# The place of the value products in TensorE's queue, in the head loop of three fused attentions

## The chip, the cores and the metric

One core of one Trainium2 chip runs the whole program. The metric is the device time of one execution in microseconds, as the median of the runs. All times below that belong to one moment are microseconds from the start of the profiled execution's span.

## What is computed

A first block of two layers (short convolution and SwiGLU; dilated-group attention and a mixture of experts), and behind it a second block of two layers, on 256 tokens of width 1024, all in float32. The change lies in the attentions, of which there are three: one with 15 heads in the first block, and one with 16 heads in each layer of the second. Cut to one head, each computes:

```python
s = einsum('qd,kd->qk', q, k) * HEAD_DIM ** -0.5   # 256 x 256, head dimension 64
s = s + bias_or_mask                                # window, T5 table, neighbourhood, or causal dilation
p = softmax(s)                                      # (second block: six heads with a sink logit)
o = einsum('qk,kd->qd', p, v)
```

In the first block all heads are causal, so the first 128 queries need one tile of 128 keys and the others two. In the second block both query tiles have two key tiles. After the heads come a scaling, in the second block an RMS norm for each of three groups of heads, and the output projection.

## The kernel before

The program is written engine by engine, with an explicit queue for each (TensorE, ScalarE, VectorE, GpSimd, SyncE) and semaphores between them; nothing reorders it. What counts here is the function `attention` of TensorE, and the two functions of the same name of ScalarE and VectorE that work against it. Heads go in pairs p = 0, 1, ..., 7; the 16 heads of the second block go in the order 10, 1, 0, 11, 12, 3, 2, 13, 14, 5, 4, 15, 6, 7, 8, 9. Tiles are held two deep, one for each head of a pair: `ps` banks 4 and 5 for scores, `prob` for probabilities, `ps` banks 6 and 7 for transposed probabilities, `probT` for their copy in SBUF. Value products go to `ps` banks 0 to 3, where all heads' outputs stay until they are scaled.

TensorE, in turn p, issues: the scores of pair p (line 933; waits for `s_max`, the maxima of pair p-1), the transposes of pair p-1 (line 945; waits for `s_exp`, and for `s_pte` of the pair before it, since the bank is used again), and the value products of pair p-2 (line 960; waits for `s_pte`, the copy to SBUF).

ScalarE, in turn p: four exponentials (line 1410; waits for `s_max` of its head), in the first five turns the high half of one weight unit (line 436), then the two copies of the transposes (line 1422; each waits for `s_ptp`, the transposes of its head, and for `s_pv`, the value products of the head two before, which read the same `probT`). In the last turn of the second block's attentions there stand the exponential of the sinks (line 1641) and two square sums (line 1635) ahead of the copies.

VectorE, in turn p: for each head a pass over each query tile (line 1927) that adds scores and bias, writes `prob` and takes the maximum (waits for `s_sc_ps`, the scores, and for `s_ptp`, the transposes of the head two before, which read the same `prob`); for heads 0 to 3 of the second block a mask pass (line 1908) stands ahead of it. Then one or two accumulations of a later layer's modulation (line 1733), and in turns 1 to 5 the low half of one weight unit (line 440). After the last turn VectorE reduces the head statistics, scales the heads (lines 2103, 2342; waits for `s_pv`), and normalizes (from line 2355). SyncE issues the bias loads of a head four biased heads ahead, after `s_max`.

Of the kernel before, what the change touches and what calls it, by code (L numbers as in the profile page):

```python
# [24 lines left out]
P = 128  # L25
S = 256
T = S // P
# [175 lines left out]
def build(nc, g, out, ctx):  # L203
# [3 lines left out]
    def sem(name):  # L207
        return ctx.enter_context(nc.semaphore(name))
# [43 lines left out]
    prob = prob_both[:, 0:2 * T * S].rearrange("p (i t s) -> p i t s", i=2, t=T)  # L252
# [33 lines left out]
    ps = ctx.enter_context(nc.psum_tensor("ps", [P, 8, 512], F32))  # L286
    ident = table[:, C_ID:C_ID + P]
# [49 lines left out]
    s_sc_ps, s_max, s_exp = sem("scores_in_psum"), sem("max_ready"), sem("exp_done")  # L337
    s_ptp, s_pte, s_pv = sem("probT_in_psum"), sem("probT_out"), sem("pv_in_psum")
# [194 lines left out]
    def _(sp):  # L533
# [5 lines left out]
        def mods(n):  # L539

            for q in range(mod_at[0], mod_at[0] + n):
                m, _, k, third = MOD_ORDER[q]
                w = mod_source(m)[0]
                if q >= MOD_SLOTS:
                    sp.wait_ge(s_mused, q - MOD_SLOTS + 1)
                sp.dma_start(mod_in[:, q % MOD_SLOTS, :], w[k * P:(k + 1) * P, third * MOD_W:(third + 1) * MOD_W])\
                    .then_inc(s_min[q % MOD_SLOTS], 16)
            mod_at[0] += n
# [160 lines left out]
    def head_list(second):  # L709

        heads = []
        if not second:
            for h in range(H1):
                heads.append((h // 2, h % 2, 8 + h // 2, h % 2, 2 * W1 + h * HD))
            return heads
        for h in range(4):
            heads.append((h // 2, h % 2, 2 + h // 2, h % 2, 512 + h * HD))
        for grp, (c0, v0) in enumerate(((4, 1280), (8, 1920))):
            for h in range(6):
                kv = h // 3  # L720
                same = kv == h % 2
                heads.append((c0 + h // 2, h % 2, c0 + 3 if same else 12 + grp, h % 2, v0 + kv * HD))
        return heads

    def key_tiles(second, qt):
        return T if second or qt else 1


    def head_order(second):

        return HEAD_ORDER if second else tuple(range(H1))
# [10 lines left out]
    def _(pe):  # L742
# [167 lines left out]
        def beside_later(order, j):  # L910

            later = [h for h in order[j + 1:] if h // 8 == order[j] // 8]
            if order[j] + 1 in later:
                return 0, 1
            return (1, 0) if order[j] - 1 in later else (0, 0)

        def attention(a):

            second = a > 0
            heads, order = head_list(second), head_order(second)  # L920
            n, i0 = len(heads), HEADS_BEFORE[a]
            pe.wait_ge(s_qte, TRANS_BEFORE[a] + TRANS[a] // 2)
            width = QKV2 if second else QKV1
            pairs = (n + 1) // 2
            pair = lambda p: range(2 * p, min(2 * p + 2, n)) if 0 <= p < pairs else ()
            for p in range(pairs + 2):
                if p and p < pairs:
                    pe.wait_ge(s_max, i0 + 2 * p)
                for qt in range(T):
                    for i in pair(p):  # L930
                        qc, qh, kc, kh, _ = heads[order[i]]
                        nk = key_tiles(second, qt) * P
                        last = pe.matmul(ps[:, 4 + i % 2, qt * S:qt * S + nk],  # L933
                                         qkT[qh * HD:(qh + 1) * HD, qc, qt * P:(qt + 1) * P],
                                         qkT[kh * HD:(kh + 1) * HD, kc, 0:nk], start=True, stop=True)
                        if qt == T - 1:
                            last.then_inc(s_sc_ps, 1)
                for j in pair(p - 1):
                    pe.wait_ge(s_exp, i0 + j + 1)
                    if j >= 2:  # L940
                        pe.wait_ge(s_pte, i0 + j - 1)
                    for qt in range(T):
                        for kt in range(key_tiles(second, qt)):
                            at = (qt * key_tiles(second, 0) + kt) * P
                            last = pe.transpose(ps[:, 6 + j % 2, at:at + P],  # L945
                                                prob[:, j % 2, qt, kt * P:(kt + 1) * P], ident)
                    last.then_inc(s_ptp, 1)
                for j in pair(p - 2):
                    pe.wait_ge(s_pte, i0 + j + 1)
                    if second and j == n - 2:  # L950
                        pe.wait_ge(s_ho, 6 * (a - 1) + 2)
                    h = order[j]
                    v = heads[h][4]
                    left, right = beside_later(order, j)
                    for qt in range(T):
                        dst = ps[:, 2 * qt + h // 8, (h % 8 - left) * HD:(h % 8 + 1 + right) * HD]
                        nk = key_tiles(second, qt)
                        for kt in range(nk):
                            at = kt * width + v
                            last = pe.matmul(dst, probT[:, j % 2, qt * key_tiles(second, 0) + kt, :],  # L960
                                             qkv[:, at - left * HD:at + (1 + right) * HD],
                                             start=kt == 0, stop=kt == nk - 1)
                    last.then_inc(s_pv, 1)

        def y_transposes(a, first, end):

            for pair in range(first, end):
                pe.wait_ge(s_y, Y_BEFORE[a] + Y_READY[a][pair])
                for i in range(2):
                    c = Y_CHUNK(a, 2 * pair + i)  # L970
                    w = o_rows(c) if a == 0 else P
                    for t in range(T):
                        at = i * S + t * P
                        last = pe.transpose(ps[0:w, 4 + pair, at:at + P], xn[:, t, c * P:c * P + w], ident)
                last.then_inc(s_yTp, 1)
# [168 lines left out]
        pe.wait_ge(s_qa, 6)  # L1144
        pe.wait_ge(s_qd, 6)
        attention(0)
        y_transposes(0, 0, 4)
        project_out(fa, N_WO1, O_CHUNKS, o_rows, lambda k: (s_yTl, k + 1))
# [5 lines left out]
        for c in range(DC):  # L1154
            pe.wait_ge(s_htl, HT(3) + c + 1)
            pe.matmul(ps[0:2 * E, 0, 0:S], rw[:, c, :], hTh[:, c, :], start=c == 0, stop=False)
            last = pe.matmul(ps[0:2 * E, 0, 0:S], rw[:, c, :], hTl[:, c, :], start=False, stop=c == DC - 1)
# [14 lines left out]
        for t in range(T):  # L1172
            last = pe.matmul(ps[:, 1, t * E:(t + 1) * E], act[0:2 * E, 0, t * P:(t + 1) * P],
                             table[0:2 * E, C_ST:C_ST + E], start=True, stop=True)
# [79 lines left out]
        for l in range(2):  # L1254
            n0 = l * LAYER_UNITS
            s = 4 + 2 * l
            if l == 0:
                sum_cols(s)
            normed_T(s)
            q0, d0 = 6 + 4 * l, 6 + 3 * l  # L1260

            def first_pairs():
                pe.wait_ge(s_htl, HT(s + 1))
                pe.wait_ge(s_qa, q0 + 3)
                pe.wait_ge(s_qc, l + 1)
                qk_transposes(1 + l, 0, 3)

            project_in(fb, n0 + N_IN2, 4, 512, s, q0, d0, {(3, 2): first_pairs})
            sum_gate(s)
            pe.wait_ge(s_q, 3 + l)  # L1270
            qk_transposes(1 + l, 3, 6)
            pe.wait_ge(s_qa, q0 + 4)
            pe.wait_ge(s_qd, d0 + 3)
            qk_transposes(1 + l, 6, 7)
            pe.wait_ge(s_mga, s + 1)
            attention(1 + l)
            y_transposes(1 + l, 0, 2)
            project_out(fb, n0 + N_WO2, DC, lambda k: P, lambda k: (s_yTl, 2 * YT0[1 + l] + k + 1),
                        free=(s_ho, 6 * (l + 1)), beside=lambda: y_transposes(1 + l, 2, 4))
            sum_cols(s + 1)  # L1280
            normed_T(s + 1)
            first_ht = HT(s + 1)
            dense(fb, n0 + N_FFN2, l * STEPS, s + 1)
# [1138 lines left out]
```

## Time and profile before

| what | us |
|---|---|
| median of 3 runs | 1982.87 (1980.46 to 1987.34) |
| span of the profiled execution | 1978.7 |
| TensorE busy in the span | 1862.4 (94%) |
| VectorE busy | 1638.0 (83%) |
| ScalarE busy | 1141.5 (58%) |

The page gives no time for the profiled execution other than its span. A span runs from the first to the last recorded instruction; the device time of a run is somewhat longer. In the rows below PE is TensorE's matmul, PEld its weight load, DVE is VectorE, ACT ScalarE; L933 is line 933 of the kernel; `out<-in` are the tiles. In a timeline, the bracket at the end tells how long the engine sat idle before the instruction and who released it, and xN that N instructions of one line stand merged in it.

### The profile page before, as it was taken

The page shows a single profiled execution, that of the slowest core. Times are in us where ns is not written, and L with a number is a line of the kernel's source. Part 1 is how long each engine was busy: PE and PEld are TensorE (multiplying, and loading weights), DVE is VectorE, ACT ScalarE, POOL GpSimd, SP SyncE. Part 2 cuts the span into 40 slices and gives each one's busy share as a digit, 9 for nine tenths or more (in the row PEclk, how much of TensorE's full clock was granted, in tenths as well). Part 3 has the DMA queues.
Part 4 walks back from the last instruction along what each step waited for, and adds up shares of the span by engine and source line. Part 5 has one row for each costly group of instructions (what it writes and reads, how often), then busy time and mean ns, then how long its engine had stood idle before and what let it go on. Part 6 is the DMA issues. An engine that isn't in the chain of part 4 may idle for free.

```text
span 1978.7 us, 32211 instructions
## 1 busy us (share of the span) xinstructions
PE 1862.4 (94%) x10670; PEld 1603.6 (81%) x10670; DVE 1638.0 (83%) x2193; ACT 1141.5 (58%) x1616; POOL 36.1 (2%) x47
## 2 busy tenths in 40 slices
PE   3999998988999999999999999988799998889998
PEld 2989998866788888888888888866689997679997
DVE  7999995768999999999999989887887758887554
ACT  3445444454777777777777777754654435545443
POOL 2000000000000000000000000000000000000000
PEclk9999999999999999999999999988999999999999
DMA  9978995557799999999999999958478874845772
GB/s 326 352 250 308 384 365 154 172 177 244 261 343 359 344 361 341 359 341 360 341 361 341 360 341 359 339 191 244 142 234 279 283 262 148 245 159 189 224 222 80
DMA packets 368485, 551.26 MB, mean 279 GB/s; under 512 B 35827, under 2 KB 293110, under 8 KB 368342
## 3 DMA queue, kind: packets, MB, share of 16 engines
q1 hardware_dynamic: 365392, 547.81, 82.3%
q10 hardware_dynamic: 2118, 1.46, 0.3%
q8 instruction: 65, 1.06, 0.2%
q14 instruction: 78, 0.64, 0.1%
q0 software_dynamic: 832, 0.30, 0.1%
HBM read 548.38 MB, written 1.08 MB: 278 GB/s over the span
## 4 chain that ended last, share of the span: by engine, by line
PE 84%; DVE 9%; ACT 3%; issue 2%; DMA 1%; POOL 0%; DVEq 0%; ACTq 0%; POOLq 0%
PE ps L445 25%; PE ps L447 25%; PE ps L446 25%; ACT prob L1410 2%; PE ps L960 2%; PE ps L1193 2%; DVE units_low L440 1%; DVE mod_acc L1733 1%; PE ps L1068 1%; PE ps L945 1%; DVE x_tokens L1760 1%; PE ps L796 1%; DVE x_normed L1759 1%; PE ps L771 1%; PE ps L933 1%
## 5 line engine op out<-in xcount | busy, mean ns | idle before, releaser
L440 DVE TENSOR_TENSOR units_low<-raw_units,units_high 128x1024 fp32r<-128x1024 f32 (+1 forms) x838 | 982.7, 1218 | 144.9 <-ACT units_high L436 142.1
L436 ACT ACTIVATE units_high<-raw_units 128x1024 fp32r<-128x1024 f32 (+1 forms) x838 | 846.3, 1057 | 300.0 <-PE ps L447 267.8
L445 PE MATMUL ps<-units_high,hT_high 128*128 128x512 f32 (+1 forms) x1040 | 412.1, 396 | 1.6 <-DVE hT_low L2161 1.4
L447 PE MATMUL ps<-units_high,hT_low 128*128 128x512 f32 (+1 forms) x1040 | 408.8, 393 | 0.0
L446 PE MATMUL ps<-units_low,hT_high 128*128 128x512 f32 (+1 forms) x1040 | 405.9, 390 | 0.0
L445 PE MATMUL ps<-hT_high,units_high 128*128 128x256 f32 x1248 | 346.3, 277 | 6.5 <-DVE hT_low L1802 5.2
L446 PE MATMUL ps<-hT_low,units_high 128*128 128x256 f32 x1248 | 345.5, 277 | 0.0
L447 PE MATMUL ps<-hT_high,units_low 128*128 128x256 f32 x1248 | 345.5, 277 | 0.0
L445 PE MATMUL ps<-units_high,aT_high 128*128 128x512 f32 x632 | 255.1, 404 | 1.2 <-DVE qkT L1997 0.6
L447 PE MATMUL ps<-units_high,aT_low 128*128 128x512 f32 x632 | 248.7, 393 | 0.0
L446 PE MATMUL ps<-units_low,aT_high 128*128 128x512 f32 x632 | 247.1, 391 | 0.0
L445 PEld LDWEIGHTS ps<-hT_high,units_high 128*128 128x128 f32 x1248 | 235.0, 188 | 8.7 <-issue 6.0
L446 PEld LDWEIGHTS ps<-hT_low,units_high 128*128 128x128 f32 x1248 | 235.2, 188 | 1.1
L447 PEld LDWEIGHTS ps<-hT_high,units_low 128*128 128x128 f32 x1248 | 235.0, 188 | 0.0
L445 PEld LDWEIGHTS ps<-units_high,hT_high 128*128 128x128 f32 x1040 | 197.0, 189 | 46.2 <-issue 3.3
L447 PEld LDWEIGHTS ps<-units_high,hT_low 128*128 128x128 f32 x1040 | 196.4, 189 | 43.1
L446 PEld LDWEIGHTS ps<-units_low,hT_high 128*128 128x128 f32 x1040 | 196.8, 189 | 42.3 <-issue 0.2
L1733 DVE SCALAR_TENSOR_TENSOR mod_acc<-mod_in,silu_c,mod_acc 128x1024 f32<-128x1024 f32 x168 | 213.9, 1280 | 9.5 <-DMA mod_in<-in_mod_w 3.7
L447 PEld LDWEIGHTS ps<-units_high,aT_low 128*128 128x128 f32 x632 | 118.7, 188 | 25.7
L445 PEld LDWEIGHTS ps<-units_high,aT_high 128*128 128x128 f32 x632 | 118.9, 188 | 24.4 <-issue 1.7
L446 PEld LDWEIGHTS ps<-units_low,aT_high 128*128 128x128 f32 x632 | 119.0, 188 | 23.7 <-issue 1.0
L1388 ACT ACTIVATE gu_silu<-ps 128x256 f32<-128x256 f32 x88 | 33.8, 384 | 145.0 <-PE ps L447 145.0
(283 smaller groups left out, 1430.2 us busy)
## 6 DMA issues: line engine op xcount, KB each, us to landing
raw_units<-in_moe_w_gate SPq DMA_DIRECT2D x352, 256.0 KB, 4.5
raw_units<-in_moe_w_up SPq DMA_DIRECT2D x352, 256.0 KB, 5.8
raw_units<-in_moe_w_down SPq DMA_DIRECT2D x176, 512.0 KB, 6.3
mod_in<-in_mod_w SPq DMA_DIRECT2D x96, 512.0 KB, 6.8
mod_in<-in_w_mod SPq DMA_DIRECT2D x96, 512.0 KB, 5.4
raw_units<-in_w_gu SPq DMA_DIRECT2D x176, 256.0 KB, 3.8
raw_units<-in_w_down SPq DMA_DIRECT2D x44, 512.0 KB, 4.2
raw_units<-in_w_in SPq DMA_DIRECT2D x32, 512.0 KB, 6.8
```

Source lines behind the costliest of these rows:

```text
L436: eng.activation(whi[:rows, high_slot(f, n), 0:width], raw[:rows, raw_slot(f, n), 0:width], ACT.Copy).then_inc(f.hi, 1)
L440: eng.tensor_tensor(low[:rows, raw_slot(f, n), 0:width], raw[:rows, raw_slot(f, n), 0:width], whi[:rows, high_slot(f, n), 0:width].bitcast ...
L445: pe.matmul(dst, ah, bh, start=start, stop=False, **kw)
L446: pe.matmul(dst, ah, bl, start=False, stop=False, **kw)
L447: return pe.matmul(dst, al, bh, start=False, stop=stop, **kw)
L771: last = pe.matmul(ps[:, bank + half, :], ones, gate_acc(m)[:, half * 512:(half + 1) * 512], start=True, stop=True)
L796: last = pe.transpose(ps[:, 4 + b, at:at + P], xn[:, t, c * P:(c + 1) * P], ident)
L960: last = pe.matmul(dst, probT[:, j % 2, qt * key_tiles(second, 0) + kt, :], qkv[:, at - left * HD:at + (1 + right) * HD], start=kt == 0, s ...
L1193: last = pe.matmul(ps[:, 2 + c // 4, (c % 4) * P:(c % 4 + 1) * P], xn[:, t, c * P:(c + 1) * P], hot[:, t, :], start=t == 0, stop=t == T - 1)
L1388: ac.activation(gu_silu[:, 0:tiles, :], ps[:, b:b + tiles, 0:FW], ACT.Silu).then_inc(f.silu, 1)
L1410: last = ac.activation(prob[:, i % 2, qt, 0:nk], prob[:, i % 2, qt, 0:nk], ACT.Exp, bias=negm(qt, h), scale=-1.0, accum_out=sums(qt, h))
L1733: ve.scalar_tensor_tensor(out=acc, in0=mod_in[:, q % MOD_SLOTS, :], scalar=silu_c[:, at:at + 1], in1=acc, op0=ALU.mult, op1=ALU.add).then_ ...
```

## The change

In TensorE's `attention`, the block that issues the value products of pair p-2 is put in front of the block that issues the transposes of pair p-1. Both are unchanged in themselves, with the waits that they had. In a turn TensorE now issues: scores of p, value products of p-2, transposes of p-1. The order within ScalarE, VectorE and SyncE is unchanged. It applies to all three attentions.

```diff
-                for j in pair(p - 1):
-                    pe.wait_ge(s_exp, i0 + j + 1)
-                    if j >= 2:
-                        pe.wait_ge(s_pte, i0 + j - 1)
-                    for qt in range(T):
-                        for kt in range(key_tiles(second, qt)):
-                            at = (qt * key_tiles(second, 0) + kt) * P
-                            last = pe.transpose(ps[:, 6 + j % 2, at:at + P],
-                                                prob[:, j % 2, qt, kt * P:(kt + 1) * P], ident)
-                    last.then_inc(s_ptp, 1)
                 for j in pair(p - 2):
                     pe.wait_ge(s_pte, i0 + j + 1)
                     if second and j == n - 2:
...
                                              qkv[:, at - left * HD:at + (1 + right) * HD],
                                              start=kt == 0, stop=kt == nk - 1)
                     last.then_inc(s_pv, 1)
+                for j in pair(p - 1):
+                    pe.wait_ge(s_exp, i0 + j + 1)
+                    if j >= 2:
+                        pe.wait_ge(s_pte, i0 + j - 1)
+                    for qt in range(T):
+                        for kt in range(key_tiles(second, qt)):
+                            at = (qt * key_tiles(second, 0) + kt) * P
+                            last = pe.transpose(ps[:, 6 + j % 2, at:at + P],
+                                                prob[:, j % 2, qt, kt * P:(kt + 1) * P], ident)
+                    last.then_inc(s_ptp, 1)
```

## Rows read from the trace of the kernel before

**Rows 1.** The page: its span, and the shares of the chain by engine.

```profile
span 1978.7 us, 32211 instructions
...
PE 84%; DVE 9%; ACT 3%; issue 2%; DMA 1%; POOL 0%; DVEq 0%; ACTq 0%; POOLq 0%
```

**Rows 2.** Stretches of the three attentions: length, busy time by engine, PEclk, DMA share, GB/s.

```profile
416.00:450.00 34.00, 24.81 (x194) 18.99 (x194) 31.38 (x88) 25.46 (x82) 2.29 (x2) 1.00 0.59 184
1368.00:1418.00 50.00, 37.88 (x256) 31.01 (x256) 36.40 (x91) 33.63 (x94) 0.00 (x0) 0.86 0.70 220
1702.00:1749.00 47.00, 36.09 (x256) 29.70 (x256) 36.19 (x91) 33.21 (x93) 0.00 (x0) 0.93 0.73 221
```

**Rows 3.** The chain that ended last, second attention: start, length, what.

```profile
1389.69 2.07 ACT prob L1410 x8
...
1391.81 0.66 PE ps L945 x4
1392.47 1.80 PE ps L960 x16
...
1394.84 2.07 ACT prob L1410 x8
```

**Rows 4.** Timeline of PE, second and third attention: start, length, instruction, idle before.

```profile
1380.33 1.83 PE L945 MATMUL ps<-table,prob 128*128 128x128 f32 x8
...
1392.30 1.95 PE L960 MATMUL ps<-qkv,prob 128*128 128x128 f32 x16
1394.18 1.13 PE L933 MATMUL ps<-qkT 64*128 64x256 f32 x8
...
1710.91 1.13 PE L933 MATMUL ps<-qkT 64*128 64x256 f32 x8 [1.02 <-DVE head_stats L1927]
1711.97 1.22 PE L945 MATMUL ps<-table,prob 128*128 128x128 f32 x8
```

**Rows 5.** Timeline of DVE in the second attention.

```profile
1381.59 0.42 DVE L1927 CUSTOM_DVE_ANT_0 prob<-ps,act 128x256 f32<-128x256 f32 x1 [0.99 <-PE ps L945]
...
1382.48 0.69 DVE L1908 SCALAR_TENSOR_TENSOR gu_silu<-qkv,masks 128x512 f32<-128x512 f32 x1
...
1383.90 1.28 DVE L1733 SCALAR_TENSOR_TENSOR mod_acc<-mod_in,silu_c,mod_acc 128x1024 f32<-128x1024 f32 x1
1385.10 1.22 DVE L440 TENSOR_TENSOR units_low<-raw_units,units_high 128x1024 fp32r<-128x1024 f32 x1
...
1392.64 0.48 DVE L1927 CUSTOM_DVE_ANT_0 prob<-ps,masks,small 128x256 f32<-128x256 f32 x1 [0.23 <-PE ps L945]
...
1401.99 0.48 DVE L1927 CUSTOM_DVE_ANT_0 prob<-ps,qkv,small 128x256 f32<-128x256 f32 x1
...
1403.76 2.48 DVE L1733 SCALAR_TENSOR_TENSOR mod_acc<-mod_in,silu_c,mod_acc 128x1024 f32<-128x1024 f32 x2
```

**Rows 6.** Timeline of ACT at the end of the second attention.

```profile
1412.20 0.20 ACT L1641 ACTIVATE head_weights<-head_weights 128x12 f32<-128x12 f32 x1
```

**Rows 7.** Timeline of DVE at the end of the second attention.

```profile
1413.03 1.02 DVE L2342 TENSOR_TENSOR x_normed<-ps,head_weights 128x384 f32<-128x384 f32 x2
1416.41 1.29 DVE L2342 TENSOR_TENSOR x_normed<-ps,head_weights 128x512 f32<-128x512 f32 x2 [2.36 <-PE ps L960]
...
1418.35 0.17 DVE L2355 TENSOR_SCALAR sum_squares<-sum_squares 128x4 f32<-128x4 f32 x1 [0.18 <-ACT qkT L1635]
```

**Rows 8.** Timeline of PE in the first attention.

```profile
423.27 1.50 PE L960 MATMUL ps<-qkv,prob 128*128 128x128 f32 x12
424.70 0.93 PE L933 MATMUL ps<-qkT 64*128 64x128 f32 x8
```

**Rows 9.** Timeline of PE, second attention, beside falls of the clock.

```profile
1372.39 2.08 PE L933 MATMUL ps<-qkT 64*128 64x256 f32 x8 [2.57 <-DVE head_stats L1927]
...
1411.37 0.66 PE L945 MATMUL ps<-table,prob 128*128 128x128 f32 x4 [1.72 <-ACT prob L1410]
```

**Rows 10.** Busy time of one slice of 1 us (columns as in rows 2).

```profile
1413.00:1414.00 1.00, 1.00 (x7) 1.00 (x6) 0.97 (x2) 0.38 (x1) 0.00 (x0) 0.50 0.19 78
```

## The prediction

> **What bounds the kernel now.** Read three views in this order. The page first: the span is 1978.7 us, and TensorE holds 84% of the chain that ended last [rows 1]. That is a share over the whole program, and its big lines are products of the feed-forward and expert stages, which the diff does not touch. So the second view is the busy time of the three stretches in which the edited loop runs: some 34, 50 and 47 us, together 131 us or 6.6% of the span [rows 2]. In the first, VectorE is busy for 31.38 of 34 us: the loop there is nearly VectorE's. In the second and third no engine is full (TensorE 37.88 and VectorE 36.40 of 50 us), so a chain of waits across engines sets the pace. The third view is that chain in the middle of the second stretch [rows 3]: ScalarE does the four exponentials of a pair, TensorE the transposes of its second head, then at once all value products of the pair before, and only after these ScalarE copies the transposes out and begins the next pair's exponentials. From one pair's exponentials (1389.69) to the next (1394.84) are 5.15 us. The copy waits for the value products since it overwrites the buffer (two heads deep) from which they read.
>
> I call a pair's scores S, VectorE's bias-and-maximum passes M, exponentials E, transposes T, copies C, value products V. Waits in the code: S(p+1) waits for M(p); M(p+1) of a head waits for T(p) of the same head, since both use one probability buffer; T waits for E; C for T and for the V of the pair before; V for C.
>
> **What the change does to that chain.** TensorE's queue goes from S(p+1), T(p), V(p-1) to S(p+1), V(p-1), T(p). No instruction is added or removed, no wait is new, no DMA is issued in this block. V(p-1) needs only copies that are already out, so it now runs while ScalarE still does E(p), and C(p) no longer waits for it. This takes V out of the chain of [rows 3]. What is late next? T(p) now comes last in a turn, and M(p+1) waits for it. S(p+2), first in the next turn, waits for M(p+1). Before, those M passes ran beside V(p-1), which stood behind T(p); now nothing of TensorE's stands between T(p) and S(p+2), and TensorE sits idle through M. The new ring is S, V, T of one head, M of two heads, S.
>
> Its length, from rows. S to the next block on TensorE when nothing waits: 1710.91 to 1711.97, 1.06 us [rows 4]. V, start to next start: 1392.30 to 1394.18, 1.88 us [rows 4]. T of the first head to its end: 0.66 us, and from the end of a T (1391.81 + 0.66) to the M that waited for it (1392.64) 0.17 us [rows 3, 5]. M of two heads: one takes 0.69 us (the start of the mask pass 1382.48 + 0.69 + 0.04, to the next work at 1383.90), a biased one 0.82, so 1.39 for two plain ones; the pair of two biased heads took 1401.99 to 1403.76, 1.77 us, with its gap between them [rows 5]. End of M to S: 0.06 us, like the 0.05 from the end of E (1389.69 + 2.07) to T (1391.81) [rows 3]. Sum: 1.06 + 1.88 + 0.66 + 0.17 + 0.06 + (1.39 to 1.77) = 5.22 to 5.60 us, against 5.15 before. In one turn of each later stretch (heads 12 and 3) the mask pass of the second head stands inside M: 1381.59 to 1383.90, 2.31 us [rows 5], and the turn is 6.14 us. The other two sides of the ring are shorter and give nothing: ScalarE (four exponentials 2.07 [rows 3]; a split and two copies, about 1 each) needs some 4 us; VectorE's work between two M blocks (one accumulation 1.28 or two 2.48, one split 1.22) is at most 3.7 us [rows 5], and between M's end and the next M lie 0.06 + 1.06 + 1.88 + 0.66 + 0.17 = 3.83 us. The biased heads' loads are issued by SyncE once the M of four biased heads before is done, and are wanted two turns, some 10 us, later; they and the accumulations' loads shift with M and have that room.
>
> So the loop in the two later stretches is not quicker but a little slower. Walking the second stretch: V(0) starts where T(1) did, at 1380.33 [rows 4], at half rate until the clock comes back near 1382 (that T took 1.83 instead of 1.22 us); T(1) from about 1382.9, M(2) 1383.75 instead of 1381.59, S(3) 1386.1. Then S(4) 1391.3, S(5) 1396.8, S(6) 1402.3, S(7) 1407.9, end of the last M 1413.5, last exponentials, half of 2.07 later, 1414.5. VectorE still has one accumulation and a small sum to do, so the sink exponential, at 1412.20 before [rows 6], comes at about 1414.9: **2.7 us later**. Walking the third stretch from S at 1710.91, where the clock is full at once, gives 2.6 us.
>
> **The tail gives most of it back.** Before, VectorE scaled heads 10 to 15 at 1413.03 and then waited 2.36 us for the value products behind the last transposes, to scale the first eight heads at 1416.41 [rows 7]. Afterwards V(6) has been done during the last exponentials, and that wait is gone: heads 10 to 15 stand 0.83 us behind the sink exponential as before (1412.20 to 1413.03), at 1415.75, and take 1.02 us; the first eight follow at 1416.8, 0.4 us later than before. What is late next is ScalarE's square sum behind its last two copies, which puts the root chain (1418.35 before [rows 7]) at about 1419.1. The last V follows those copies and ends before the first output transpose wants TensorE. Net cost: **+0.75 us** in the second stretch and, in the same way, **+0.65 us** in the third.
>
> **First stretch.** S takes 0.93 us there, V 1.43 from its start to the next (423.27 to 424.70) [rows 8], T of one head less than the 0.66 above; with 0.17 and 0.06 some 3.2 us lie between M's end and the next M. With two accumulations and a split (2.48 + 1.22 = 3.7 us, three turns) VectorE covers this. With one accumulation and a split (2.5) or two accumulations alone (2.48), three turns in all, about 0.7 us of VectorE idleness shows, of which some was there before. In the tail the last copy comes earlier, but the sums on VectorE come later. Bounds: -0.4 (only the earlier copy counts) to +1.5 us; near the middle, as both are real: **+0.5 us**.
>
> Sum: 0.5 + 0.75 + 0.65 = +1.9 us on the span of 1978.7, so 1980.6. That execution's own time outside the span is not shown; the median of the runs, 1982.87, lies 4.2 us above the span, and I carry that over: **1984.8 us**. The three runs spread over 1980.46 to 1987.34, so of this kernel a measurement can tell about 0.3%, 6 us, from no change. Mine is a third of that.
>
> **Clock.** TensorE's granted clock is the cost that I can't place exactly. A wait of 2.57 us was followed by a stretch at 1.2 GHz, in which S took 2.08 us instead of about 1.13, and one of 1.72 us with little work around it likewise [rows 9]: clock 0.50 in the slice from 1413 [rows 10]. The new wait of S, from the end of both heads' T (1.22 us after its start [rows 4]), is 0.66 + 0.17 + M + 0.06 - 1.22: 1.1 to 1.4 us in most turns and 2.0 in the one with the mask pass. In the first stretch TensorE was busy for only 24.81 of 34 us and kept a clock of 1.00 [rows 2]; the new turns have 4.0 of 5.22 to 5.60 us, a like share, so I take the clock as kept. The page "TensorE: Matmul & The Clock Gate" of the Trainium skill, section "Part 1: The HAM clock gate", says that the throttled state is the default and that activity releases it, which speaks against any order with idle time in every turn; the rival below gives its time here.
>
> **Rivals.**
> 1. The plain promise: T and the next S do not get in each other's way, V is hidden and nothing takes its place. The turn would be TensorE's own 1.06 + 1.88 + 1.06 = 4.0 us, or VectorE's 1.4 to 1.8 + 2.5 to 3.7: about 1 us less in six turns of two stretches, 12 us, and 2.4 us in each tail: about 1966 us. For it: the copy's wait does vanish. Against: the wait of S for M, and of M for T, are both in the code. Chance 0.04.
> 2. The ring is as long as the old one (the drain and M overlap more than I added up), and the tails gain their 2.36 us: 1982.87 - 4.7 = 1978.2. Chance 0.12.
> 3. One fall of the clock in each later stretch, at the 2.0 us gap: S and V at half rate for one slow stretch, some 1.7 us each, 3.4 in all: 1988.2. For it: 2.0 lies between waits that were followed by falls. Chance 0.17.
> 4. Slower: the clock falls again and again, since each turn now has its idle time in one piece. S is then 2.08 instead of 1.13 and V, by the same ratio, near 3.5 instead of 1.88; with T a turn costs some 3.2 us more. Were half of the 12 later turns low, +19 us: 2004. It decides from the point at which 1.1 to 1.4 us of idleness in 5.4 is too much; against it stands the first stretch's 1.00. Chance 0.07.
> The forecast itself has 0.60.
>
> **How the numbers follow.** The likeliest case gives 1984.8. The range takes in rival 2 (down to 1978.2, with its upper part), rival 3 and the first stretch's bounds, and leaves out rivals 1 and 4 and some of the spread at each end: 1979 to 1990. Faster by over 0.3% (below 1976.9): rival 1 and a sliver of 2, 0.05. Slower by over 0.3% (above 1988.8): rival 4 and part of 3, 0.12. Within: 0.83.
>
> **What would show it.** Right: in the chain of waits of the two later stretches the pieces are V, T, VectorE's bias-and-maximum passes, S; TensorE's idle time before the scores' line is 1.1 to 1.4 us, released by VectorE; ScalarE no longer waits for value products; turns of 5.2 to 5.6 us; VectorE goes from heads 10 to 15 to the first eight without a wait. Wrong: turns near 4 us (rival 1), or scores at over 2 us in the middle of the loop (rivals 3 and 4). The prediction fails if M starts before T of its head has ended, or if the loop's stretches move by more than 3 us each.

## The result and the profile after

| | before | after |
|---|---|---|
| median of 21 runs each, us | 1984.62 (1979.02 to 1992.57) | 1993.13 (1985.1 to 1999.72) |
| span of the profiled execution, us | 1978.7 | 1987.7 |

The ratio is 1.0037, 95% interval 1.0023 to 1.0050: the change makes the kernel slower, by 7.3 us (4.6 to 9.9), where I had forecast 1.9 us, no measurable change and at most 1990. The sign is the one of the sum; its size is not.

The page of the changed kernel, its span and busy times. No instruction was added (32211 before too), and TensorE's busy time grew by 5.4 us, more than nothing:

```profile
span 1987.7 us, 32211 instructions
...
PE 1867.8 (94%) x10670; PEld 1610.4 (81%) x10670; DVE 1639.3 (82%) x2193; ACT 1144.6 (58%) x1616; POOL 36.1 (2%) x47
```

The three stretches of the attentions (length, then busy time of PE, PEld, DVE, ACT and POOL, PEclk, DMA share, GB/s), beside [rows 2]. The first no longer has a clock of 1.00:

```profile
415.50:450.50 35.00, 25.00 (x191) 19.97 (x190) 30.56 (x81) 25.15 (x81) 2.29 (x2) 0.95 0.53 167
1370.50:1421.00 50.50, 35.79 (x253) 30.19 (x253) 37.52 (x100) 33.16 (x95) 0.00 (x0) 0.91 0.66 215
1708.50:1759.00 50.50, 35.96 (x254) 30.31 (x255) 37.54 (x101) 33.15 (x95) 0.00 (x0) 0.91 0.68 209
```

The chain that ended last, in the middle of the second attention. Where [rows 3] had exponentials, transposes, value products and copy, it now has S (L933), V (L950), T of the first head (L961), M (L1927), S. ScalarE is gone from it:

```profile
1391.24 1.13 PE ps L933 x8
1392.38 1.98 PE ps L950 x16
1394.36 0.45 PE ps L961 x4
...
1394.94 0.38 DVE prob L1927
...
1396.12 0.40 DVE prob L1927
...
1396.58 1.13 PE ps L933 x8
```

The timeline of PE in the same attention, beside [rows 4]. From S to S: 6.15 us in the turn with the mask pass, then 5.25, 5.34, 6.77 and 5.49. Every wait of S is for VectorE. In the turn of 6.77 us V took 3.03 instead of 2.05 and T 1.75 instead of 1.04, without any wait inside:

```profile
1379.84 1.13 PE L933 MATMUL ps<-qkT 64*128 64x256 f32 x8 [1.35 <-DVE head_stats L1927]
...
1385.99 1.13 PE L933 MATMUL ps<-qkT 64*128 64x256 f32 x8 [2.16 <-DVE head_stats L1927]
...
1391.24 1.13 PE L933 MATMUL ps<-qkT 64*128 64x256 f32 x8 [1.26 <-DVE head_stats L1927]
1392.31 2.05 PE L950 MATMUL ps<-qkv,prob 128*128 128x128 f32 x16
1394.19 1.04 PE L961 MATMUL ps<-table,prob 128*128 128x128 f32 x8
1396.58 1.13 PE L933 MATMUL ps<-qkT 64*128 64x256 f32 x8 [1.35 <-DVE head_stats L1927]
1397.65 3.03 PE L950 MATMUL ps<-qkv,prob 128*128 128x64 f32 x16
1400.47 1.75 PE L961 MATMUL ps<-table,prob 128*128 128x128 f32 x8
1403.35 1.14 PE L933 MATMUL ps<-qkT 64*128 64x256 f32 x8 [1.13 <-DVE head_stats L1927]
...
1408.84 1.14 PE L933 MATMUL ps<-qkT 64*128 64x256 f32 x8 [1.50 <-DVE head_stats L1927]
```

The clock explains that turn: slices of 1 us of the same stretch (PEclk is the third number from the end) show it at 0.50, 1.2 GHz, from 1398.5 on (the slice from 1398 has 0.75). It fell behind a wait of 1.35 us, three turns after the one of 2.16 us that the prediction had feared, and with value products running.

```profile
1397.00:1398.00 1.00, 1.00 (x11) 0.65 (x8) 1.00 (x2) 1.00 (x5) 0.00 (x0) 1.00 0.77 293
1398.00:1399.00 1.00, 1.00 (x9) 1.00 (x9) 0.86 (x1) 0.81 (x1) 0.00 (x0) 0.75 0.43 92
1399.00:1400.00 1.00, 1.00 (x6) 1.00 (x6) 0.00 (x0) 0.00 (x0) 0.00 (x0) 0.50 0.42 78
```

The first and the third attention have one such turn each. PE in the first, behind waits of 1.72 and 1.76 us, where VectorE came late with two accumulations and a split:

```profile
433.96 0.93 PE L933 MATMUL ps<-qkT 64*128 64x128 f32 x8 [1.72 <-DVE head_stats L1927]
...
438.79 1.15 PE L933 MATMUL ps<-qkT 64*128 64x128 f32 x8 [1.76 <-DVE head_stats L1927]
439.87 2.93 PE L950 MATMUL ps<-qkv,prob 128*128 128x128 f32 x12
```

The tail of the second attention went as summed: VectorE scales all heads in one piece (the 1.02 and 1.29 us of [rows 7] without the 2.36 between them), 0.84 us behind the sink exponential. Timeline of ACT and DVE:

```profile
1415.54 0.21 ACT L1641 ACTIVATE head_weights<-head_weights 128x12 f32<-128x12 f32 x1
```

```profile
1416.38 2.22 DVE L2342 TENSOR_TENSOR x_normed<-ps,head_weights 128x384 f32<-128x384 f32 x4
...
1419.56 0.17 DVE L2355 TENSOR_SCALAR sum_squares<-sum_squares 128x4 f32<-128x4 f32 x1 [0.49 <-ACT qkT L1635]
```

**Where the 9.0 us between the two profiled executions are.** I compared the start of each matmul instruction in one with the start of the same instruction in the other. The lag is -0.4 us at the head of the first attention, 2.7 behind it and all through the experts, 2.2 behind the second attention, 6.6 at the end of the dense layer that follows, and 9.0 behind the third. So 4.4 us arose in a layer that the change does not touch. There the pace of matmuls of 256 columns differs: 48 instructions from 1500.01 to 1505.45 before (113.3 ns each), 48 from 1503.77 to 1509.42 after (117.7 ns), at a granted clock of 1.00 in both. The experiments begin with that.

### The profile page after: what moved, and what is told of

Read it like the earlier page. It is cut to its first block, busy times and chain, and to the rows that moved or that the text cites. A ratio compares the mean times of both kernels' runs of the same rounds, so it can differ in the third digit from the quotient of the medians.

```text
span 1987.7 us, 32211 instructions
## 1 busy us (share of the span) xinstructions
PE 1867.8 (94%) x10670; PEld 1610.4 (81%) x10670; DVE 1639.3 (82%) x2193; ACT 1144.6 (58%) x1616; POOL 36.1 (2%) x47
## 3 DMA queue, kind: packets, MB, share of 16 engines
q8 instruction: 65, 1.06, 0.2%
## 4 chain that ended last, share of the span: by engine, by line
PE 84%; DVE 11%; issue 2%; ACT 2%; DMA 0%; POOL 0%; DVEq 0%; ACTq 0%; POOLq 0%
PE ps L445 25%; PE ps L447 25%; PE ps L446 24%; PE ps L950 2%; DVE units_low L440 2%; PE ps L1193 2%; DVE mod_acc L1733 2%; PE ps L933 1%; DVE prob L1927 1%; PE ps L1068 1%; DVE x_tokens L1760 1%; DVE x_normed L1759 1%; PE ps L771 1%; PE ps L961 1%; DVE act L1798 1%
```

## The experiments

All ratios are to the kernel before, run on the same chip, with 95% intervals. For the loops I use two lengths from each profile, taken between matmul instructions, the same for all kernels: the **loop**, from the first to the last scores instruction of an attention, and the **tail**, from there to the 320th matmul instruction counted from the first scores (it takes in the first part of the output projection). Helper functions shift line numbers in some kernels: there L962 (or L950, L955) is a value product and L946 (L961, L966) a transpose.

**The kernel before, against itself.** No edit.

> The kernel before, unchanged, against itself. What is open is 4.3 us of the 9.0 us between the two profiled executions: in the first dense layer of the second block every matmul started 117.8 ns after the last instead of 113.5, at a granted clock of 1.00 in both, in code that the change does not touch. Theory A: that pace is chance of an execution, and has nothing to do with the change; then some dense layer of this kernel's execution may show it too, and the ratio is 1.000 within 0.0015. Theory B: the pace comes from the change (where it leaves TensorE when the layer begins); then this kernel's profile shows 113.5 ns in all three dense layers, as the one before did.

Ratio 0.9994 (0.9982 to 1.0006). Its profile has the slow pace too: in the first dense layer of the second block the first 193 matmuls of 256 columns start 117.8 ns after one another, the rest of that layer and the two other layers run at 113.5. So theory A holds already here, with no edit at all. Timeline of PE; from the first to the last row are 18 instructions, 2.12 us:

```profile
1461.81 0.28 PE L445 MATMUL ps<-hT_high,units_high 128*128 128x256 f32 x1
...
1463.93 0.28 PE L445 MATMUL ps<-hT_high,units_high 128*128 128x256 f32 x1
```

**The change in the first attention only.**

```diff
+                if second:
+                    transposes(pair(p - 1))
+                    values(pair(p - 2))
+                else:
+                    values(pair(p - 2))
+                    transposes(pair(p - 1))
```

> The value products in front of the transposes in the first attention only; the two later ones as before. Between the start of the scores and the first matmul of the output projection the first attention took 39.34 us before and 42.33 with the change, of which two low stretches of the clock explain some 3 us. Theory A (the ring T, M, S, V has its idle time in one piece of 1.7 us where VectorE is late, and the clock falls once in the loop and for longer behind it): +2 to +3 us, ratio 1.001 to 1.0015. Rival (only the ring, 0.5 us, the falls are chance): ratio 1.0003.

Ratio 1.0011 (0.9992 to 1.0030), 2.2 us: in the middle of theory A, though the interval takes in the rival and no change at all. Its first attention met the same waits as in the changed kernel, 1.71 and 1.76 us, and its clock did not fall inside the loop. Its profile, of 1994.2 us, had the slow pace already in the first block's dense layer, which lies before every attention and is the same code in the same place as before. Timeline of PE there; from the first to the last row are 18 instructions, 2.12 us, 117.8 ns each:

```profile
200.51 0.28 PE L446 MATMUL ps<-hT_low,units_high 128*128 128x256 f32 x1
...
202.63 0.28 PE L446 MATMUL ps<-hT_low,units_high 128*128 128x256 f32 x1
```

The same 18 in the kernel before took 2.04 us, 113.3 ns each:

```profile
200.51 0.28 PE L445 MATMUL ps<-hT_high,units_high 128*128 128x256 f32 x1
...
202.55 0.28 PE L445 MATMUL ps<-hT_high,units_high 128*128 128x256 f32 x1
```

So the pace does not come from the change: it is a matter of the single execution, some 4.3 us for each dense layer that has it. It also appeared in a kernel below that was 17 us faster (the one with the deep tile). It widens the runs' spread and makes a single pair of spans useless for a difference of this size.

**The change in the two later attentions only.**

```diff
+                if second:
+                    values(pair(p - 2))
+                    transposes(pair(p - 1))
+                else:
+                    transposes(pair(p - 1))
+                    values(pair(p - 2))
```

> The change in the two later attentions only. Theory A: turns of 5.2 to 6.2 us instead of 5.15 and one fall of the clock within each loop, 2 to 2.5 us each after what the tail gives back: +4 to +5 us, ratio 1.0022. Rival (only the ring as summed before the result, 0.7 us each): +1.4 us, ratio 1.0007. If the sum of this and of the first attention alone stays well under the 7.3 us of the whole change, something else is in it.

Ratio 1.0029 (1.0007 to 1.0050), 5.8 us. Together with the first attention 1.0040, against 1.0037 for the whole: the parts add up as far as intervals of 0.2% either way can tell. Its second attention is rival 4 of the prediction in one instance: the clock came back only inside the third turn and fell again. Timeline of PE, three turns with V at 3.78 us twice:

```profile
1378.98 3.78 PE L962 MATMUL ps<-qkv,prob 128*128 128x128 f32 x16
1382.55 1.21 PE L946 MATMUL ps<-table,prob 128*128 128x128 f32 x8
1385.91 1.75 PE L933 MATMUL ps<-qkT 64*128 64x256 f32 x8 [2.16 <-DVE head_stats L1935]
1387.59 3.78 PE L962 MATMUL ps<-qkv,prob 128*128 128x64 f32 x16
```

**The change with a probability tile four heads deep.** It cuts the wait of M for T, and touches nothing else of the order.

```diff
+    prob_more = xn[:, 0, :].rearrange("p (i t s) -> p i t s", i=2, t=T)
+
+    def prob_slot(j):
+        return (prob_more if j % 4 < 2 else prob)[:, j % 2]
...
-                    if i >= 2:
-                        ve.wait_ge(s_ptp, i0 + i - 1)
+                    if i >= 4:
+                        ve.wait_ge(s_ptp, i0 + i - 3)
```

> The change, and the probability tile four heads deep instead of two (two more heads' worth lie in the token tile, which is free then), so that VectorE's passes for a head wait for the transposes of the head four before. If the ring T, M, S, V is the cause, it is cut: M(p+1) runs beside V(p-1) and T(p), the turn is what TensorE (4.0 us), ScalarE (4.1) or VectorE (4.0 to 5.2) needs, about 4.5 us instead of 5.15 before, and the tails keep their 2.4 us: 5 to 6 us less than before in each later attention, nothing in the first, ratio 0.9945. If the loss has another cause (the clock, the order itself), the ratio stays at 1.002 to 1.004.

Ratio 0.9915 (0.9897 to 0.9933), 1970.11 us: **17 us faster than before**, the ring was the cause. I had expected 11. The profile has the rest: 1.3 us less in the first loop, where I had expected nothing, and in each later attention 4.4 us less in the loop and 3.2 in the tail than the means of the old order further down. Turns are 3.92 us, TensorE's own S, V and T without a wait (timeline of PE; S is L938, V L955, T L966):

```profile
1383.34 1.13 PE L938 MATMUL ps<-qkT 64*128 64x256 f32 x8
1384.40 2.05 PE L955 MATMUL ps<-qkv,prob 128*128 128x64 f32 x16
1386.29 1.04 PE L966 MATMUL ps<-table,x_normed 128*128 128x128 f32 x8
1387.26 1.13 PE L938 MATMUL ps<-qkT 64*128 64x256 f32 x8
```

**The deep tile with the old order.** Same edit on the kernel before.

> The four-deep probability tile with TensorE's order as before the change (transposes, then value products). It tells whether the gain of the deep tile with the new order (ratio 0.9915) is the tile's own. Theory A: in the old order the ring runs through exponentials, transposes, value products and copies, and M is beside it, so that a deeper tile buys nothing in turns of 5.15 us: ratio 0.998 to 1.001. Rival (M was late in the old order as well and its wait for the transposes cost most): ratio below 0.995, and then the order has little part in the gain.

Ratio 1.0002 (0.9984 to 1.0019). The tile alone gives nothing; the order alone costs 0.37%; both together give 0.85%. Each hides the other's wait: the old ring ran through V and the copy, the new one through M and S.

**Head by head.** V and T of a turn alternate by head, so that M of the first head runs beside the second half.

```diff
+                old, new = pair(p - 2), pair(p - 1)
+                for k in range(2):
+                    values(old[k:k + 1])
+                    transposes(new[k:k + 1])
```

> The two blocks of a turn taken head by head: value products of head 0, transposes of head 0, value products of head 1, transposes of head 1. M of head 0 then runs beside the second half. By the ring: 1.06 (S) + 0.94 + 0.53 + 0.94 + 0.66 + 0.17 + 0.69 to 0.82 (M of head 1 alone) + 0.06 = 5.05 to 5.18 us, the old 5.15, and 5.9 in the turn with the mask pass; V stays off ScalarE's path, so the tails keep their gain of some 2 us each. TensorE's waits are 0.8 us shorter and the clock should hold. Ratio 0.997 to 1.000. Rival (any order with T last costs the same, since S waits for M): ratio 1.003.

Ratio 0.9993 (0.9976 to 1.0010), and a turn of 4.92 us (1399.99 to 1404.91) where I had summed 5.05 to 5.18; the neighbouring ones have 5.12 and 5.15. Timeline of PE:

```profile
1399.99 1.14 PE L933 MATMUL ps<-qkT 64*128 64x256 f32 x8 [1.13 <-DVE head_stats L1933]
1401.05 1.11 PE L962 MATMUL ps<-qkv,prob 128*128 128x64 f32 x8
1402.00 0.61 PE L946 MATMUL ps<-table,prob 128*128 128x128 f32 x4
1402.44 1.06 PE L962 MATMUL ps<-qkv,prob 128*128 128x128 f32 x8
1403.33 0.60 PE L946 MATMUL ps<-table,prob 128*128 128x128 f32 x4
1404.91 1.14 PE L933 MATMUL ps<-qkT 64*128 64x256 f32 x8 [0.98 <-DVE head_stats L1933]
```

It is faster than the changed kernel (the intervals 0.9976 to 1.0010 and 1.0023 to 1.0050 are apart), so V ahead of T as such is not what costs; what costs is both heads' T behind both heads' V.

**Filling TensorE's wait.** Matmuls behind T, from the second turn to the last but one, whose result is used nowhere.

```diff
+                if 1 <= p <= pairs - 2:
+                    free = order[2 * p]
+                    for _ in range(8):
+                        pe.matmul(ps[:, free // 8, free % 8 * HD:(free % 8 + 1) * HD], ident,
+                                  table[:, 0:HD], start=True, stop=True)
```

> The change, and behind the transposes of each turn from the second to the last but one eight more matmuls of 64 columns on a place in PSUM that the next value products overwrite (their result is used nowhere): about 0.94 us of work in the 1.1 to 2.0 us in which TensorE waits for M. Theory: the ring is as long as with the change, but the clock no longer falls within the loops; that gives back 1.4 to 1.7 us for each fall in a loop, of which the profile of the changed kernel had three: ratio to the kernel before 1.001 to 1.002 instead of 1.0037, turns of 5.25 to 6.2 us at a clock of 1.00 in the profile. Rival (falls are no part of the average loss, or the added matmuls delay S): ratio 1.0035 or more.

Ratio 1.0048 (1.0019 to 1.0078). A miss by my own sizing: each of these matmuls is two instructions, the filling took 1.90 us and not 0.94, longer than the wait, and S came late. Behind the head of the loop all turns are 5.65 us at full clock:

```profile
1400.91 1.04 PE L961 MATMUL ps<-table,prob 128*128 128x128 f32 x8
1401.78 1.90 PE L967 MATMUL ps<-table 128*128 128x64 f32 x16
1403.61 1.13 PE L933 MATMUL ps<-qkT 64*128 64x256 f32 x8
```

**The filling, halved**, four matmuls instead of eight.

> The filling again at half the size: a float32 matmul of this kernel is two instructions in the trace, so eight of them were 16 of 0.1175 us, 1.9 us and longer than the wait of 1.1 to 1.5 us that they were to fill; the turns became 5.65 us. Now four, 0.94 us, in the turns from the second to the last but one, results used nowhere. Theory (a part of the loss is the clock): turns as with the change, none at half rate inside the loops but for the fall that the start brings; from the first to the last scores 37.0 to 37.5 us in the later attentions instead of 37.9 to 43.6, and the ratio 0.001 to 0.0015 below that of the changed kernel in this call. Rival (the clock's falls add nothing on average): the same ratio as the changed kernel within 0.0005.

**The changed kernel again**, beside it on the same chip. No edit.

> The changed kernel once more, beside the other two of this call. Ratio 1.0037 as before, 1.002 to 1.005. In the profile I expect from the first to the last scores 38 us in the later attentions (35.5 is the mean of eight such loops in the old order) and, from there to the 320th matmul instruction counted from the first scores, 29.2 to 31 us (31.2 in the old order).

Ratios 1.0015 (0.9994 to 1.0036) with the filling, 1.0036 (1.0015 to 1.0056) without: the difference of 0.0021, 4 us, is what the clock theory wants and four times the rival's bound, but the two intervals overlap, so the times alone don't show it.

The granted clock, which is on record for every run as a mean over its span, says more. On this chip it is 0.9812 over the 12 filled runs, 0.9783 over the 10 unfilled ones and 0.9813 over 27 of the kernel before; filled less unfilled is 0.0029, with a standard error of 0.0011. The changed kernel's first 21 runs have 0.9776, and the kernel before has 0.9818 and 0.9821 in the two other groups. So the change gives up some clock in its runs generally and not only in the profiled ones, and the short filling gives it back. The long filling did so only in part: 0.9801, where the kernel before had 0.9821.

The profile of the filled kernel does its part: turns of 5.25 to 5.5 us like the ring's, the wait of S down to some 0.5 us, no turn at half rate once the start's slow stretch is over.

```profile
1403.43 1.04 PE L961 MATMUL ps<-table,prob 128*128 128x128 f32 x8
1404.31 1.00 PE L967 MATMUL ps<-table 128*128 128x64 f32 x8
1405.82 1.13 PE L933 MATMUL ps<-qkT 64*128 64x256 f32 x8 [0.51 <-DVE head_stats L1932]
```

Its first attention's loop is 28.50 us (29.47 and 29.66 in the changed kernel's two profiles, which have a fall there; but 28.50 also in the unfilled a2_first, which has none), its third's 37.04. Over all profiles the clock fell inside the loop, behind its head, in five of nine changed attentions without filling and in none of six with it. The second's, 39.33, missed my 37.0 to 37.5: the start's slow stretch lasted 10.2 us instead of 3.4, and there the filling ran at half rate.

**The new order in the last turn only**, where there are no scores any more.

```diff
+                if p == pairs:
+                    values(pair(p - 2))
+                    transposes(pair(p - 1))
+                else:
+                    transposes(pair(p - 1))
+                    values(pair(p - 2))
```

> The value products in front of the transposes only in the turn that has no scores any more (behind the last pair's exponentials); in all other turns the old order. By the parts: the loops stay at the old 35.5 us, no M waits behind this turn, and the tails keep what the whole change gained there: 31.2 us less 1.5 to 2.4 in each of the two later attentions, 0 to 0.5 in the first. Ratio 0.998 to 0.999. Rival (the tail's gain exists only because the loop before it was late): ratio 1.000.

Ratio 0.9982 (0.9962 to 1.0003), as the parts said, though the interval just reaches no change. The tails are 30.29 and 30.34 us, 0.9 less than the old mean of 31.2 and not the 1.5 to 2.4 I wanted; V stands alone behind a wait of 2.26 us there and met the clock at half rate (3.17 instead of 2.00 us):

```profile
1411.67 3.17 PE L962 MATMUL ps<-qkv,prob 128*128 128x128 f32 x16 [2.26 <-DVE x_normed L2350]
```

**The deep tile, and the head of the loop filled** (18 and 10 such matmuls in turns 0 and 1 of the later attentions, sized with the mistake above).

> The change with the four-deep tile (ratio 0.9915), and in the first two turns of the two later attentions, where TensorE waits 2.6 and 1.5 us for VectorE, 18 and 10 matmuls of 64 columns whose result is used nowhere, against the fall of the clock there (6.8 to 10.2 us at 1.2 GHz at the head of each, in which S takes 2.08 us instead of 1.13). If the clock holds: 2 to 4 us less in each of the two, ratio 0.989. If a fall comes anyway, the fillers run at half rate, 3.8 us instead of 2.1, and delay S: ratio 0.992 to 0.993.

Ratio 0.9930 (0.9906 to 0.9955): no better than without. The granted clock rose to 0.9842, from 0.9798 with the deep tile alone, and the time did not follow. The fillers were twice as long as meant; that they took what the clock gave is how I read it, and no run separates the two.

## Why the prediction was wrong, step by step

Means over all profiles of attentions in the old order (before, a1_control, b1_deep_old, the untouched attentions of a2_first and a3_later, and for the first also c3_last_turn, whose last turn alone has the new order: without it the tail's mean is the same) and in the new one (after, c2_changed, the changed attentions of a2_first and a3_later):

| us | old order | new order | difference | predicted |
|---|---|---|---|---|
| first: loop | 27.54 | 29.21 | +1.7 | |
| first: tail | 39.62 | 40.46 | +0.8 | +0.5 for both |
| each later one: loop | 35.50 | 38.99 | +3.5 | +3.4 |
| each later one: tail | 31.22 | 29.24 | -2.0 | -2.7 |
| sum, all three | | | +5.5 | +1.9 |

The predicted loop is S(7), 1407.9 for 1404.48; the tail is the net 0.7 less that. The sum of the means, 5.5 us (1.7 and 0.8 for the first attention, twice 1.5 for the later ones), lies in the measured 4.6 to 9.9; eight loops of the old order and six of the new, with so uneven a clock, can't place it better.

- **The ring S, V, T, M, S: right.** Its pieces, its releasers and its length (5.22 to 5.60 us, 6.14 with the mask pass) stand in the chain and the timeline as 5.25, 5.34, 5.49 and 6.15. The deep tile proved the cause by taking it away. The plain promise (rival 1) was what that cut gave, not what the change gave.
- **"so I take the clock as kept": the step that failed.** It put the clock's term at nothing. I compared busy shares (4.0 of 5.4 us, and 24.81 of 34 us at a clock of 1.00), and counted rivals 3 and 4 apart, with 0.24 together. In place of a kept clock the runs show 0.9776 and 0.9783 against 0.9813 to 0.9821: 0.003 to 0.0045 of 1985 us, or 6 to 9 us of full clock given up in each execution. That is a bound on what it can cost; the filling gave the clock back and some 4 us with it, which leaves 3.0 us (-1.2 to 7.1), and the rest of my sum, 1.9, lies in that. The changed kernel's profile has one slow turn in each of the three attentions, and the repeat another mix. In the two later ones that is the picture of rival 3, though not at its place: no fall came at the 2.16 us wait. What one costs: later attentions in which the clock came back early at the head took 33.84 us on average in the old order (33.86, 33.67, and 34.06 and 33.75 in c3_last_turn), 36.87 in c2_changed with no slow turn in the loop, and 38.20 and 38.45 with one. So of the later loops' loss the ring is 3.0 us, and a slow turn adds 1.3 to 1.6; that the table's 3.5 meets my 3.4 is in part luck. In the first attention the same comparison is 28.50 without and 29.47 to 29.66 with.
- **The first stretch: sized too small, +0.5 us for a measured +2.5.** Without any slow turn it lost 1.0 us in the loop (28.50 against 27.54), in two turns (3.54 to 4.19 and 4.41 to 4.83 us), and the tail took nothing back. VectorE's cover in the turns with two accumulations was real (no full turn is longer than the old order's 4.83 us), but there TensorE now waited 1.72 and 1.76 us in one piece, and right behind these waits the clock fell in two of the three profiles with the change; in a2_first the same waits had no fall behind them, so the wait alone does not decide it. I had looked at those turns only for VectorE's sake. The tail's +0.8 goes with the clock too: all three of these profiles have a stretch at 0.50 behind the loop, of the five in the old order only three.
- **The tail: right mechanism, a part of it lost again.** Measured from the last S to the root chain (L2355), it shrank from 13.87 (1404.48 to 1418.35) to 10.72 us (1408.84 to 1419.56), 3.15, where my sum had 11.2 us (1407.9 to 1419.1), 2.7. But the old tail had V(6) and V(7) in one stream of 5.16 us, and the clock was back at full before its end; in the new one V(7) stands alone behind a wait of 2.39 us, at half rate (3.37 us), and the projection starts at half rate too. Measured past that point the gain is 2.0.
- **The range** took the clock as a rival of 3.4 us at most in its inside. The changed kernel's median, 1993.13, lies above 1990 also because the median of the kernel before was 1984.62 over 21 runs and not 1982.87 over three.

What stays open: how much of the 7.3 us is the clock. The filling gives 4 us. The table gives 0.7 us of slow turns in the first loop, 0.5 in each later one and 0.8 in the first tail, 2.5 in all, and 4.8 if the 1.15 us that each later tail lost again (3.15 less 2.0) are the clock's as well. In the 31 runs of the changed kernel 0.001 less clock went with 1.06 us more time (standard error 0.27), which makes 3 to 5 us of the 0.003 to 0.0045; this is an estimate from a correlation. None of the three is sharp enough to exclude half of 4 us. Nor does any run show why the same waits are followed by a fall in one execution and not in the next.

## What to carry to other kernels

When a reorder takes work off the chain of waits, write down the whole ring that remains, engine by engine, with its buffer depths: here the order and the depth of one tile were each worth nothing or less alone and 17 us together. Don't take TensorE's clock as kept from a busy share. In an old turn of the later attentions TensorE waited 0.66 and 0.33 us, in a new one 1.1 to 2.2 us in one piece, and the clock fell inside the loops; whether the piece or the sum of the waiting does it, no run here separates. And read the clock from many executions, in all stages: the mean granted clock of each run showed the loss, while one profile has a fall and the next, with the same waits, has none.

## What the runs showed of the hardware that I had not expected

- Matmuls of 256 columns run at one of two paces, 113.5 or 117.8 ns from start to start, at the same granted clock of 1.00, for a whole dense layer at a time (some 170 us) or for its first 193 matmuls (a1_control, a2_first, b1_deep_old, b3_split), and changing from layer to layer and from execution to execution of the same code. It is worth 4.3 us a layer. No run here shows what chooses it.
- The clock at the head of the later attentions, after a wait of 2.56 or 2.57 us in each profile that has no filling there, stays at 1.2 GHz for anything from about 3 to 14 us in different executions. With it loops of the old order took from 33.67 us (3.4 us at 1.2 GHz) to 36.56 us (10.2 us).
- A filling of matmuls that nobody reads, in a wait that stays, kept the clock up: 0.9812 with it and 0.9783 without, on the same chip. The page "TensorE: Matmul & The Clock Gate" of the Trainium skill (section "Part 1: The HAM clock gate") says that activity releases the throttle; the trace with the halved filling agrees in that it has no turn at half rate after the head of the loop.
